# Two models in one kernel: a new order of the seven products and output products in pairs

## The reference

```
first block, per layer:
    h = h + 0.5 * swiglu(rms_norm(h, ffn1_norm), ffn1_w_in, ffn1_w_out)
    u = rms_norm(h, mix_norm);  (z_s, xbc, dt_s, qkv, z_d, ..., gate_s, gate_d) = split(u @ w_in)
    y_s = mamba2_branch(...)     # state space, 32 heads of 64, chunks of 128
    y_d = deltanet_branch(...)
    h = h + (sigmoid(gate_s) * (y_s @ ssm_w_branch) + sigmoid(gate_d) * (y_d @ dn_w_branch)) @ w_out
    h = h + 0.5 * swiglu(rms_norm(h, ffn2_norm), ffn2_w_in, ffn2_w_out)
state space, per head:   seg = a_cum[l] - a_cum[s];  decay = exp(seg) where causal
    y = (cb * decay) @ xdt;  y = (y + xs * d_skip) * silu(z);  y * rsqrt(mean(y*y) over a group of 8 heads)
second block, per layer: u = rms_norm(h); (q, k, v, g, c_in, gates) = split(u @ w_in); retention, a gated
    convolution, cross attention to a memory, and conv_ffn (products up and down), each added to h
```

## Time and profile before

| | us |
|---|---|
| median of 3 runs | 3251.45 (3251.38 to 3257.51) |
| the profiled execution | 3251.46 |
| its span | 3249.6 |
| TensorE matmul busy | 3227.2 |
| VectorE busy | 2288.5 |
| ScalarE busy | 631.1 |
| DMA, mean over the span | 153 GB/s |

### The profile page before, as it was taken

The page is one execution under the profiler, slowest core; times in us unless marked ns, Lnnn a source line. Parts: engine busy times, 40 slices in busy tenths (PEclk is TensorE's granted clock), DMA queues, the critical chain, the costliest instruction groups (busy, mean ns, idle before and its releaser), DMA issues.

```text
span 3249.6 us, 58141 instructions
## 1 busy us (share of the span) xinstructions
PE 3227.2 (99%) x24518; PEld 3045.5 (94%) x24518; DVE 2288.5 (70%) x5121; ACT 631.1 (19%) x1431; POOL 268.5 (8%) x338
## 2 busy tenths in 40 slices
PE   9999999999999999999999999999999999999998
PEld 8999889899999998898999999979999999889998
DVE  5657577376666575764766798877786898876785
ACT  1113232211111132322211111211211111212211
POOL 0202000001102020000011000200022000200031
PEclk9999999999999999999999999999999999999999
DMA  5444344344444443443544444344344444343453
GB/s 190 169 157 144 132 139 144 110 168 169 169 161 169 157 144 132 140 145 108 192 169 158 154 169 169 128 148 156 130 169 169 168 169 169 119 153 123 166 169 130
DMA packets 89637, 497.42 MB, mean 153 GB/s; under 512 B 25088, under 2 KB 29600, under 8 KB 30368
## 3 DMA queue, kind: packets, MB, share of 16 engines
q1 hardware_dynamic: 70608, 489.45, 44.1%
q10 hardware_dynamic: 18768, 4.25, 0.6%
HBM read 491.55 MB, written 2.11 MB: 152 GB/s over the span
## 4 chain that ended last, share of the span: by engine, by line
PE 90%; DVE 7%; ACT 2%; issue 1%; DMA 0%; ACTq 0%; DVEq 0%
PE bank L342 83%; DVE arena L1484 1%; PE bank L500 1%; DVE arena L990 1%; DVE arena L988 1%; DVE arena L992 1%; DVE arena L987 0%; PE bank L2651 0%; PE bank L1987 0%; PE bank L2691 0%; PE bank L2708 0%; PE bank L1956 0%; ACT arena L2287 0%; PE bank L1933 0%; DVE arena L2544 0%
## 5 line engine op out<-in xcount | busy, mean ns | idle before, releaser
L342 PE MATMUL bank<-arena 128*128 128x128 f32 x8640 | 1021.7, 275 | 0.2
L342 PEld LDWEIGHTS bank<-arena 128*128 128x128 f32 x8640 | 992.6, 192 | 1.0 <-DVE arena L992 1.0
L342 PE MATMUL bank<-arena,ring 128*128 128x128 f32 (+1 forms) x6144 | 971.1, 311 | 3.8 <-ACT arena L826 3.8
L342 PEld LDWEIGHTS bank<-arena,ring 128*128 128x128 f32 x6144 | 876.6, 191 | 64.7 <-issue 6.7
L342 PE MATMUL bank<-xT,ring 128*128 128x128 f32 (+1 forms) x5376 | 844.1, 312 | 1.3 <-DVE arena L951 1.3
L342 PEld LDWEIGHTS bank<-xT,ring 128*128 128x128 f32 x5376 | 765.5, 191 | 50.7 <-DVE arena L951 1.6
L987 DVE TENSOR_TENSOR arena<-ring 128x512 f32<-128x512 f32 x318 | 218.1, 686 | 126.9 <-PE bank L342 109.6
L943 ACT ACTIVATE arena<-bank 128x128 f32<-128x128 f32 x286 | 79.3, 277 | 1096.9 <-PE bank L342 1091.8
L1041 DVE TENSOR_TENSOR arena<-arena,bank 128x256 f32<-128x256 f32 x286 | 119.4, 418 | 204.8 <-ACT arena L943 204.0
L342 PE MATMUL bank<-xT,arena 128*128 128x128 f32 x1728 | 229.0, 275 | 2.9 <-DVE arena L992 2.7
L992 DVE TENSOR_TENSOR arena<-ring,arena 128x512 f32<-128x512 f32 x318 | 223.4, 703 | 11.0
(11 more groups left out here) (316 smaller groups left out, 2268.1 us busy)
## 6 DMA issues: line engine op xcount, KB each, us to landing
ring<-w SPq DMA_DIRECT2D x461, 1024.0 KB, 4.9
ring<-w SPq DMA_DIRECT2D x4, 256.0 KB, 6.1
hT<-hT_d ACTq DMA_DIRECT2D x4, 256.0 KB, 6.3
arena<-blocks_d ACTq DMA_DIRECT2D x4, 256.0 KB, 5.6
arena<-base_d ACTq DMA_DIRECT2D x16, 64.0 KB, 4.4
arena<-memT_d SPq DMA_DIRECT2D x1, 1024.0 KB, 8.6
outT<-hT SPq DMA_DIRECT2D x4, 256.0 KB, 2.4
arena<-dmask_d SPq DMA_DIRECT2D x1, 768.0 KB, 9.5
```

Of the source, the lines that this page charges most:

```text
L342: ins = self.e.matmul(out, lhsT, rhs, start=start, stop=stop)
```

## The change

Four parts. In `seven`, calls without a `ready` function take the products in another order and wait for the sums as each needs them; calls with one keep the old order. In the loop of the state space two output products stand in a row behind every second product, and the two spreads behind them; the lists of VectorE, ScalarE and the chain banks follow. In the second block's first layer VectorE reads c_in's first opening before the norm. SyncE waits for the last quarter of h ahead of chunk 1.

```
@@ seven (the new order)
+        def summed(n):
+            e.wait_ge(sems.sum_by_pool if f in BY_POOL else sems.sum_by_dve, 4 * SUMMED[f] + n)
         product(X, 0, lambda g: a(0, g), "B11", first, False)
         product(X, 1, lambda g: a(1, g), "B21", False, False)
+        if ready:
+            summed(4)
...
+        else:
+            product(Y, 0, lambda g: a(3, g), "T4", first, False)
+            summed(2)
+            product(X, 3, lambda g: s(3, g), "T3", False, False)
+            summed(3)
+            finished(product(X, 2, lambda g: s(2, g), "T2", False, last))
             product(Y, 1, lambda g: s(1, g), "T1", False, False)
+            summed(4)
+            finished(product(Y, 2, lambda g: s(4, g), "B22", False, last))
@@ chain_jobs
         for p in range(STEPS):
-            if p < 16:
-                spec += [((L, "y", p), "dve")]
-            if p + 3 < 16:
-                spec += [((L, "seg", p + 3), "dve")]
+            if p % 2 and p < 16:
+                spec += many(L, "y", 2, "dve", p - 1)
+                spec += [((L, "seg", n), "dve") for n in (p + 2, p + 3) if n < 16]
             if p in Y_NORM_AT:
                 spec += [((L, "y_norm", Y_NORM_AT.index(p)), "act")]
@@ first_act
-        if p + 3 < 16:
-            decay(p + 3)
+        if p % 2:
+            for n in (p + 2, p + 3):
+                if n < 16:
+                    decay(n)
@@ first_dve
         if p + 1 < 16:
             mix(p + 1)
-        if p < 16:
+        if p % 2 and p < 16:
+            y_out(p - 1)
             y_out(p)
-        if p + 3 < 16:
-            seg(p + 3)
+            for n in (p + 2, p + 3):
+                if n < 16:
+                    seg(n)
@@ first_pe
         t.product((L, *BESIDE[p]), xT)
-        if p < 16:
+        if p % 2 and p < 16:
+            for n in (p - 1, p):
+                bank = t.open_chain(L, "y", n)
...
-        if p + 3 < 16:
-            spread("seg", p + 3, 0)
+            for n in (p + 2, p + 3):
+                if n < 16:
+                    spread("seg", n, 0)
         if p in Y_NORM_AT:
@@ second_dve
+    if L == DEPTH:
+        e.wait_ge(sems.rstd_ready, 3 * L + 2)
+        tt(m.rstd_both, m.rstd_both, m.rstd, ALU.mult).then_inc(sems.dve_step, 1)
+        e.wait_ge(sems.dve_step, seen.up("dve_step"))
+        opened_by_dve(v, m, L, "c_in", m.seven_x.c[:, 0, 0, :], m.th[:, 0, :], 0, m.rstd_both)
     norm_by_dve(v, m, 3 * L + 1, cols("mix_norm", 8))
@@ before(c)
+                    if c == 1:
+                        e.wait_ge(sems.h_loaded[3], 16)
```

More of the change, by code:

```diff
@@ L395, in product, with finished @@
             return ins
+        def summed(n):
+            e.wait_ge(sems.sum_by_pool if f in BY_POOL else sems.sum_by_dve, 4 * SUMMED[f] + n)
+        def finished(ins):
+            if last:
+                ins.then_inc(sems.bulk_done, 1)
         product(X, 0, lambda g: a(0, g), "B11", first, False)
         product(X, 1, lambda g: a(1, g), "B21", False, False)
-        if f in BY_POOL:
-            e.wait_ge(sems.sum_by_pool, 4 * SUMMED[f] + 4)
-        else:
-            e.wait_ge(sems.sum_by_dve, 4 * SUMMED[f] + 4)
-        product(Y, 2, lambda g: s(4, g), "B22", first, False)
-        if new:
-            product(Y, 1, lambda g: s(1, g), "T1", False, False)
[L407 to L415, removed]
+        if ready:
+            summed(4)
+            product(Y, 2, lambda g: s(4, g), "B22", first, False)
+            if new:
+                product(Y, 1, lambda g: s(1, g), "T1", False, False)
+            product(X, 2, lambda g: s(2, g), "T2", False, False)
+            finished(product(X, 3, lambda g: s(3, g), "T3", False, last))
+            if not new:
+                product(Y, 1, lambda g: s(1, g), "T1", False, False)
+            finished(product(Y, 0, lambda g: a(3, g), "T4", False, last))
+        else:
+            product(Y, 0, lambda g: a(3, g), "T4", first, False)
[3 more added lines that the diff above has]
+            finished(product(X, 2, lambda g: s(2, g), "T2", False, last))
+            product(Y, 1, lambda g: s(1, g), "T1", False, False)
+            summed(4)
+            finished(product(Y, 2, lambda g: s(4, g), "B22", False, last))
     def opening(self, outs, done, n, again=False):
@@ L1926, in first_pe @@
         t.product((L, *BESIDE[p]), xT)
-        if p < 16:
[L1928 to L1935, removed]
-        if p + 3 < 16:
-            spread("seg", p + 3, 0)
+        if p % 2 and p < 16:
+            for n in (p - 1, p):
+                bank = t.open_chain(L, "y", n)
+                e.wait_ge(sems.mix_ready, upto(L, "mix_ready", n + 1))
+                for hh in range(2):
+                    f = (2 * n + hh) * SSM_P
+                    out = bank[hh * SSM_P:(hh + 1) * SSM_P, :]
+                    e.matmul(out[:, 0:S], m.xdt[:, 0, f:f + SSM_P], m.seg[:, n % 3, hh, 0:S], start=True, stop=False)
+                    ins = e.matmul(out[:, P:S], m.xdt[:, 1, f:f + SSM_P], m.seg[:, n % 3, hh, S:384], start=False, stop=True)
+                ins.then_inc(sems.chain_done, 1)
+            for n in (p + 2, p + 3):
+                if n < 16:
+                    spread("seg", n, 0)
         if p in Y_NORM_AT:
@@ L2359, in second_dve @@
     f = FAST_FROM[L, "c_in"]
-    if L == DEPTH:
-        tt(m.rstd_both, m.rstd_both, m.rstd, ALU.mult).then_inc(sems.dve_step, 1)
-        e.wait_ge(sems.dve_step, seen.up("dve_step"))
     n = OPENING[3 * L + 1]
     for i in range(n):
-        opened_by_dve(v, m, L, "c_in", m.seven_x.c[:, i, 0, :], m.th[:, i, :], i, m.rstd_both if L == DEPTH else None)
+        if i or L > DEPTH:
+            opened_by_dve(v, m, L, "c_in", m.seven_x.c[:, i, 0, :], m.th[:, i, :], i, m.rstd_both if L == DEPTH else None)
         if i:
```

## The result

The changed kernel takes 3262.39 us (median of 7 runs, 3261.89 to 3270.92), the kernel before 3251.45 (3249.1 to 3257.51): 1.0039 times as long, with a 95% interval of 1.003 to 1.0048. So it is slower by 10.9 us; 3260.4 was predicted, with a range of 3253 to 3265. One of the eleven executions of experiment 4 took 5435.45 us; nothing on record says why, and the ratio given there leaves it out. The profiled execution took 3262.2, its span 3260.4.

The account below looks back on a forecast made before the run. TensorE's instruction stream was taken as the bound. Costs of 14.8 (bank waits) and 5.1 (clock), 19.9, less gains 3.4 + 1.6 + 1.5 + 4.5 = 11.0, took 3251.46 to 3260.4 us; range 3253 to 3265.

Parts of the forecast that it names:

- Bank waits: State space loop, steps 7 and 11: TensorE waits 3.4 and 4.0 us ahead of y_norm, 14.8 over two layers.
- Rival (b): State space loop: VectorE reads y 6 early enough, so no bank wait and only gains, 3240.5 us; chance 0.08.
- Pairs: State space loop: paired output products save shape changes, two exits and step 14's wait; gain 4.5 us, at least 3.0.
- z_d and c_in: Waits gone at the third chunks of z_d (1.6 us, both layers) and c_in (1.5, once).
- Clock: Behind the four new y_norm gaps: three falls to half rate at 1.7 us, cost 5.1, bounds 0 and 6.8.
- rival (a): Bank waits come, but the clock stays full or falls once: 3255.3 to 3257 us; chance 0.22.
- The start: Holding chunk 1 until h is loaded brings the fourth chunk to 31.2 to 31.8 for 34.96; gain 3.4 us.
- From the norm's start the third chunk needs 8.1 us: Start: from norm to fourth chunk's start, set by token sums ending 6.6 us behind the norm's start and the last product.
- rival (c): Start gains nothing: chunk 2 lands after 23.5 or the clock falls while TensorE awaits the norm; 3263.8 us; chance 0.05.
- Up and down: Products up and down: up's wait goes, but TensorE waits longer at down's second chunk; gain 0, at most 3.5 us.
- VectorE has no pause from there to down's second chunk: From up's wait on, VectorE is continuously busy, so down's second chunk still starts when L992 ends; gain 0.
- rival (d): New product order gains in up too, as VectorE is not quite the bound there: 3.5 us, 3256.9; chance 0.03.

Follow-up runs that it names:

- experiment 4: Changed kernel with VectorE's reads of the two output products ahead of the product with the decays (mix): 3256.88 us, ratio 1.0021 to the kernel before.
- Experiment 2: Kernel before with only the output products in pairs and their spreads with them: 3269.61 us, ratio 1.0057.
- experiment 1: Changed kernel with the y_norm products of steps 7 and 11 moved to steps 6 and 10: 3248.09 us, ratio 0.9989 to the kernel before.
- 8: Changed kernel with the first two y_norm products at steps 6 and 12 instead of 7 and 11: 3243.23 us, ratio 0.9976 to the kernel before.
- Experiment 11: Kernel before with only the paired output products, and y_norm at steps 6 and 12: 3245.36 us, ratio 0.9984.
- experiment 5: Changed kernel with VectorE reading the first opening's bank ahead of chunk 2's sums and the norm: 3262.07 us, ratio 1.0032 to the kernel before.
- 9: Changed kernel with y_norm at steps 6 and 12, and the first opening's bank read, then the norm, ahead of chunk 2's sums: 3239.78 us, ratio 0.9961.
- experiment 6: Kernel before with only SyncE's wait for all of h ahead of chunk 1: 3250.76 us, ratio 1.000.
- Experiment 7: Kernel before with only the new order of the seven products: 3246.73 us, ratio 0.9989.
- 3: Changed kernel without the paired output products, the other three parts kept: 3246.38 us, ratio 0.9984 to the kernel before.
- 12: Kernel before with only c_in's opening evicted ahead of the norm: 3249.28 us, ratio 0.9994.

## Why the prediction was right, and which of its terms were not

The direction, the mechanism and the time were right (3260.4 for 3262.39), and the term that decides was right to 0.1 us. But three smaller terms were off by about 2 us each: the clock by 1.7 and the start by 2.6 one way, up and down by 2.2 the other. That the sum missed by 2 us and not by more is in part luck.

- **Bank waits**, 14.8 predicted: 3.29 + 0.10 and 3.90 + 0.10 a layer, 14.8 measured. Experiment 2 shows that part 4 alone makes them, 4 that they move with VectorE's read of y, 1 and 8 that another step for y_norm takes them away. Rival (b) is ruled out.
- **Pairs**, 4.5 predicted: the loop grew by 8.57 a layer, with 7.4 of waits and 3.4 of falls in it, so the pairs gave 2.2 a layer, 4.4. Experiment 11 confirms it without the waits.
- **z_d and c_in**, 1.6 and 1.5: both as predicted, in the traces.
- **Clock**, 5.1 predicted for three falls of four: all four came in the profiled execution, 6.8, so rival (a), with its one fall at most and 3255.3 to 3257, is ruled out. That it is four of four is a draw too, as experiments 4 and 5 show. By the Trainium skill's page TensorE: Matmul & The Clock Gate, section HAM oscillation — how this bites in real kernels, each such gap puts the engine back to half rate, and this trace and that of experiment 2 agree (8 of 8). The trace of experiment 5 doesn't: with gaps of the same length the clock fell behind 2 of 4. So it is 10 of 12 over the three profiled executions, and the rule that it happens each time is a little too strong here.
- **The start**, 3.4 predicted: 0.84 in the traces. The step that failed is "From the norm's start the third chunk needs 8.1 us". Chunk 2 (21.24, for 20.4 to 21.0) and the norm (23.77, for 23.1 to 23.7) came a little past their ranges, and the token sums end 6.6 behind the norm's start as worked out. But behind the norm on VectorE there also stands the read of the first opening's bank, and TensorE needs it to start the third chunk. In the kernel before this read ended at 26.79, and TensorE came to the third chunk at 28.71 only; 3 us earlier, TensorE came up against it. The read in the kernel before:

```profile
26.04 0.75 DVE L951 TENSOR_TENSOR arena<-bank,rstd 128x256 f32<-128x256 f32 x2
```

I had priced just this wait for c_in in part 3, and had not looked for it here. Experiments 5 and 9 show that it held the gain: moved ahead, it brings the fourth chunk to 32.23 and 31.79, near the predicted 31.2 to 31.8. The second error is one of size: the gap and the fall on which I built the term were those of an execution whose TensorE had begun at full rate. In the others there was less to gain or something to lose, and experiment 6 shows no gain in the time. Its trace also has what rival (c) named, a fall of the clock at TensorE's wait in the start, which took the gain away (35.84 for 34.96); the changed kernel's trace hasn't.
- **Up and down**, 0 predicted with an end at 3.5: 1.1 a layer, 2.2. The step that failed is "VectorE has no pause from there to down's second chunk". What came is rival (d), to which I had given 0.03, at 2.2 for its 3.5. I read the earlier trace rows at its two ends only. Between them VectorE's weight sums come at three paces. Rows of before and after in the middle of up:

```profile
2384.45 0.69 DVE L992 TENSOR_TENSOR arena<-ring,arena 128x512 f32<-128x512 f32 x1
...
2390.70 0.69 DVE L992 TENSOR_TENSOR arena<-ring,arena 128x512 f32<-128x512 f32 x1
```

```profile
2397.19 0.69 DVE L1000 TENSOR_TENSOR arena<-ring,arena 128x512 f32<-128x512 f32 x1
2403.11 0.69 DVE L1000 TENSOR_TENSOR arena<-ring,arena 128x512 f32<-128x512 f32 x1
```

5.92 us a chunk by its own work (after), 6.25 when it waits for TensorE's products (before, from 2378 to 2397), and 6.58 later, when the sums take 0.83 for 0.69 beside GpSimd's work. In the middle stretch TensorE sets the pace, so an earlier TensorE takes VectorE with it: the offset of VectorE's sums between the two traces falls from 13.37 to 12.3 there, and stays. Experiment 7 shows the same 1.1 a layer without the other parts.

With the measured terms the sum is 14.8 + 6.8 - 0.8 - 1.6 - 2.2 - 1.5 - 4.4 = 11.1, against 8.9 predicted and 10.9 measured.

## What to carry to other kernels

When work is put in pairs, go through the list that hands out the buffers again: what was filled a step before it is reused is now filled in the same step, and an engine that runs in order stands until the reader has come to it. A gain at one place ends at the next wait that still stands in the old order (here the read of the bank behind the norm). So when an engine is to run earlier, go through its next instructions one by one and ask who frees or fills what each of them needs, and what stands ahead of that. And a term read from one execution's start or clock is one draw: look at several before it is given a size.

## What the hardware showed that was not expected

- The clock doesn't follow the length of a gap alone. Behind gaps of 2.05 us it fell 2 times of 2 (experiment 1), behind 2.4 and 3.0 twice of four (4), behind 3.3 and 3.9 ten times of twelve; behind 3.4 to 3.5 us ahead of the third chunk it fell in experiment 6 and neither in 3 nor in 4. A gap of 2.2 in the same place (after) had no fall. (Each from the time at which the next matmul could have started.)
- It also fell without a gap. Behind thirty-two matmuls of 48 columns it did so in the profiles of experiments 8 (0.58 in the stretch below), 2 and 12; behind small matmuls of 32 and 64 columns in those of 9, 3, 4, 5 and 7. Each is in some executions only. Most cost the same 1.7 us; in experiment 7 the clock stayed at half for 6.8 us, and sixteen matmuls took 6.35 that take 3.72 elsewhere. So a profiled execution can be some us off its kernel's median for this alone:

```profile
1130.00:1133.40 3.40, 3.40 (x20) 3.40 (x20) 2.72 (x9) 0.57 (x2) 0.00 (x0) 0.58 0.40 89
```

```profile
1490.02 6.35 PE L342 MATMUL bank<-arena,ring 128*128 128x256 f32 x16
```

- Entering and leaving the output product's shape (64 columns of weights, 128 to 256 of data, in two halves of the array) costs 0.093 us each (the start of the next matmul comes 0.309 behind a 256-column one for 0.216); a pair of products pays both once.
